# Eleven small loads issued later, and four modulation products put together ahead of a normalisation's turning

## The reference

```
mod = silu(cond) @ w_mod[i] + b_mod[i]          # 1024 -> 6 x 1024, for two conditioning vectors
sh1, sc1, g1, sh2, sc2, g2 = split(mod, 6)
h = modulate(rmsnorm(x, norm1_g[i]), sh1, sc1)
out = hgrn_mixer(h) if i == 0 else fourier_mixer(h)
x = x + g1 * out
h = modulate(rmsnorm(x, norm2_g[i]), sh2, sc2)
x = x + g2 * moe(h)                             # 16 experts, top 2 of one group per token
```

## Time and the profile before

| | us |
|---|---|
| median of 3 runs | 1105.63 |
| lowest and highest | 1104.61, 1108.65 |
| the profiled execution | 1104.64 |
| its span in the trace | 1102.9 |

### The profile page before, as it was taken

The page is one execution under the profiler, slowest core; times in us unless marked ns, Lnnn a source line. Parts: engine busy times, 40 slices in busy tenths (PEclk is TensorE's granted clock), DMA queues, the critical chain, the costliest instruction groups (busy, mean ns, idle before and its releaser), DMA issues.

```text
span 1102.9 us, 17260 instructions
## 1 busy us (share of the span) xinstructions
PE 921.6 (84%) x6701; PEld 510.2 (46%) x6702; DVE 221.1 (20%) x509; ACT 246.4 (22%) x451; POOL 171.1 (16%) x288
## 2 busy tenths in 40 slices
PE   3699999997999965998899997399939999887850
PEld 0345546753446443554455553374425555443420
DVE  1100355201545350000010010601420100000005
ACT  1111123221224131222222221420312222211112
POOL 2001002201001032211121211210211122111112
PEclk9999999999999986999999998699959999999995
DMA  9976464556242975999999983971482999999954
GB/s 380 307 297 230 154 223 163 191 208 248 103 147 94 380 270 199 393 418 418 417 424 421 417 341 142 406 318 62 174 326 87 416 376 420 416 424 422 420 217 170
DMA packets 69227, 320.90 MB, mean 291 GB/s; under 512 B 13252, under 2 KB 15588, under 8 KB 53952
## 3 DMA queue, kind: packets, MB, share of 16 engines
q1 hardware_dynamic: 54592, 290.75, 65.9%
q0 software_dynamic: 9856, 18.51, 4.8%
q10 hardware_dynamic: 4736, 11.01, 2.6%
HBM read 308.70 MB, written 20.53 MB: 299 GB/s over the span
## 4 chain that ended last, share of the span: by engine, by line
PE 36%; DMA 23%; DVE 3%; ACT 3%; issue 2%; SPq 2%; ACTq 0%; POOLq 0%; POOL 0%; DVEq 0%
PE ps L852 13%; PE ps L859 9%; PE ps L749 7%; DMA ring<-in_moe_w_down 7%; DMA deep<-in_moe_w_down 6%; DMA deep<-hrow,gi 3%; DMA ring<-in_moe_w_up 3%; DMA hrow<-deep 2%; SPq L379 2%; DMA yrows<-deep,si 2%; PE ps L828 1%; PE ps L788 1%; PE ps L770 1%; ACT deep L943 1%; DMA deep<-yrows 1%
## 5 line engine op out<-in xcount | busy, mean ns | idle before, releaser
L852 PE MATMUL ps<-ring,deep 128*64 128x256 f32 x1600 | 184.1, 388 | 14.1 <-DMA ring<-in_moe_w_up 10.3
L852 PEld LDWEIGHTS ps<-ring,deep 128*64 128x64 f32 x1600 | 120.1, 140 | 84.7 <-issue 16.7
L571 PE MATMUL ps<-deep,ring 128*128 128x384 f32 x384 | 129.0, 494 | 4.2 <-ACT deep L943 4.2
L1414 DVE TENSOR_TENSOR deep<-deep,ps 128x128 f32<-128x128 f32 x76 | 18.4, 284 | 452.8 <-PE ps L852 452.8
L859 PE MATMUL ps<-ring,deep 128*64 128x512 f32 x400 | 94.7, 617 | 8.3 <-DVE deep L1418 8.3
L571 PEld LDWEIGHTS ps<-deep,ring 128*128 128x128 f32 x384 | 72.6, 192 | 58.9 <-issue 10.5
L852 PE MATMUL ps<-deep 128*64 128x256 f32 x832 | 92.8, 380 | 5.3 <-DMA deep<-in_moe_w_up 4.4
L574 PE MATMUL ps<-ring,deep 128*128 128x512 f32 x192 | 87.9, 610 | 0.0
L749 PE MATMUL ps<-ring,deep 128*128 128x512 f32 x192 | 83.8, 594 | 1.4 <-ACT deep L1023 0.8
L852 PEld LDWEIGHTS ps<-deep 128*64 128x64 f32 x832 | 61.0, 137 | 40.8 <-issue 6.3
L504 PE MATMUL ps<-ring,scond 128*32 128x512 f32 x384 | 52.9, 674 | 21.2 <-DMA ring<-in_w_mod 20.4
(11 more groups left out here) (162 smaller groups left out, 776.9 us busy)
## 6 DMA issues: line engine op xcount, KB each, us to landing
ring<-in_w_mod SPq DMA_DIRECT2D x24, 2048.0 KB, 12.0
ring<-in_moe_w_gate SPq DMA_DIRECT2D x22, 2048.0 KB, 22.9
ring<-in_moe_w_up SPq DMA_DIRECT2D x22, 2048.0 KB, 27.6
ring<-in_moe_w_down SPq DMA_DIRECT2D x22, 2048.0 KB, 32.7
ring<-in_hgrn_w_in SPq DMA_DIRECT2D x10, 2048.0 KB, 8.6
deep<-in_moe_w_gate SPq DMA_DIRECT2D x10, 2048.0 KB, 20.9
deep<-in_moe_w_up SPq DMA_DIRECT2D x10, 2048.0 KB, 25.2
deep<-in_moe_w_down SPq DMA_DIRECT2D x10, 2048.0 KB, 30.8
```

What stands on the lines that cost most here:

```text
L571: last = mm(bank[:, 0:T], W[:, k, b * P:(b + 1) * P], hT[:, k, :], start=(k == 0), stop=(k == KD - 1))
L852: last = mm(ps[g * SLOTS:(g + 1) * SLOTS, GU_BANK[j], 0:2 * P], xt[:, b, h * SLOTS:(h + 1) * SLOTS], slot3(S[j])[:, k, g * F // 2:(g + 1) ...
```

## The change

- `small_loads` is issued behind mod 6 instead of behind hgrn 1.
- mod 20, 21 and 22 go to slots 2, 0 and 1, which hold the weights of experts 1, 4, 7, 10 and 13, and are all issued when fourteen experts are done; mod 23 stays in slot 3 and is issued behind the DFT tables, with no wait of its own.
- The Fourier weights, which take slots 0 and 1, wait for the products of mod 21 and mod 22.
- TensorE runs the four products one after the other ahead of `turn_norm("a1")`, and none inside `fourier`.

```diff
-        for phase, u, s in [("mod", 20, 2), ("mod", 21, 3), ("mod", 22, 2), ("mod", 23, 3), ("four", 0, 0), ("four", 1, 1)]:
+        for phase, u, s in [("mod", 20, 2), ("mod", 21, 0), ("mod", 22, 1), ("mod", 23, 3), ("four", 0, 0), ("four", 1, 1)]:
             place(phase, u, s)
...
                     sp.dma_start(slot3(s), src).then_inc(landed[s], 16)
-                    if u == 1:
-                        small_loads()
                     continue
...
                 mod_load(u)
+                if u == 6:
+                    small_loads()
...
             sp.wait_ge(M[0]["used"], NE - 2)
-            sp.wait_ge(mod_mm, 20)
-            mod_load(20)
-            sp.wait_ge(M[0]["used"], NE)
-            mod_load(21)
+            for u in (20, 21, 22):
+                mod_load(u)
 
             expert_rows(0)
...
-            for U in (22, 23):
-                sp.wait_ge(mod_mm, U - 1)
-                mod_load(U)
+            mod_load(23)
             for u in range(2):
+                sp.wait_ge(mod_mm, 22 + u)
                 s, _ = plan[("four", u)]
                 sp.dma_start(slot3(s), w_o[1][0, :, :, u * C512:(u + 1) * C512]).then_inc(landed[s], 16)
...
                 for t in range(TT):
-                    if t:
-                        mod_gemv(21 + t, 3)
                     for g in range(4):
...
             experts(0)
-            mod_gemv(20, 3)
-            mod_gemv(21, 3)
+            for u in range(20, 24):
+                mod_gemv(u, 3)
             turn_norm("a1", False)
```

## The result

| | before | after |
|---|---|---|
| median, us | 1105.12 (4 runs) | 1094.29 (4 runs) |
| lowest and highest | 1104.11, 1108.65 | 1093.68, 1094.52 |
| the profiled execution | 1104.64 | 1093.68 |
| its span | 1102.9 | 1091.8 |

The ratio is 0.9896, 95% interval 0.9879 to 0.9913: about 11 us faster, where 12.2 were forecast.

A forecast was written before the change was run, and what follows sets the result against it. The chain of waits was taken as the bound, 36% of the span TensorE and 23% transfers. Terms -6.6 + 0.3 - 2.2 - 3.7 = -12.2 us from 1104.64 gave a forecast of 1092.5 us, range 1087 to 1100.

The forecast's parts named there:

- The wait for mod 4: Early projections: mod 4 issued earlier removes TensorE's 5.00 us wait and the slow clock of its product; -6.6 us.
- The small loads elsewhere: SP's queue after mod 6: the eleven small loads cost 4 to 20.3 us there, and nothing on the path.
- Gathers beside mod 21 and 22: Late in the first expert set: gathers beside the earlier loads come slightly late; +0.3 us, bounds 0 and 1.0.
- Scatter and read-back: End of first expert set: with no load issued beside them, last scatter and first read-back finish 4.27 us earlier, bounds 0 and 4.27.
- The estimate of 5.3: Last scatter beside a load, if engines alternate between queues: about twice 2.65 us, making the whole sum 1.2 us smaller.
- The hold: Before the turning: the fourth product waits for mod 23, holding the turning 3.0 us; net -2.2 us at Fourier's start.
- The products out of Fourier: Fourier stage: two products of 1.85 us each leave the chain; -3.7 us, bounds 0 and -3.7.
- rival 3: Turning and after: fourth product brings the clock up (1.7 us), mod 23 lands in time (2.1 more); 1088.7 us, chance 0.08.
- Everything behind moves along: After the early idleness: all that follows moves by its length, stretches bound by expert weights too.

The follow-up runs named there:

- the controls: The changed kernel, unaltered, rerun beside later variants: 1094.29 us (ratio to before 0.9886) and 1093.65 us (0.9898).
- start-only: The kernel before with only the small loads moved behind mod 6: 1099.02 us, ratio 0.9929.
- The two experiments on loads: Kernel before with only the end's loads moved: 1101.25 us; changed kernel with one or two loads again beside the last scatter: 1097.05 and 1099.22 us.
- loads-only: The kernel before with only mod 20 to 23's loads moved, products and small loads where they were: 1101.25 us, ratio 0.9946.

## Why the prediction was right

- **The wait for mod 4 (-6.6).** -6.5 from first to third projection. mod 4 landed 21.2 us after its issue, at 48.3 (47.4 to 48.7 forecast), ahead of 51.99. The third projection came at 53.84, not near 52.4, because the first began 1.3 us late: the third modulation product ran at the low clock (25.77 us, 3.11 for 1.92). This is not the change: three profiles of the changed kernel began their first projection at 38.13, 39.62 and 40.92.
- **The small loads elsewhere (0).** They cost SP 10.3 us, between the bounds of 4 and 20.3, and TensorE waited for neither hgrn 2 nor mod 7.
- **Gathers beside mod 21 and 22 (+0.3).** The first expert set took 249.24 us before and 250.06 after (0.65 of the difference is its first product, 9.54 for 8.89, far ahead of these loads), in the controls 249.38 and 249.76, in the start-only kernel, without these loads, 249.62. No more than a few tenths, and not told from none.
- **Scatter and read-back (-4.27, which the next term contains).** The scatter gave 4.15 (6.50 to 2.35), the read-back's first tile 0.2 (5.1 to 4.9 us to landing). The two experiments on loads show the mechanism from both sides. The Trainium skill ("DMA: Bandwidth & Descriptors", Queues, rings and completion order) has engines taking packets in turn from queues: the scatter with two loads, no longer than with one, agrees. The estimate of 5.3 made from that by equal shares is short of all readings beside one load, 6.50 to 7.29.
- **The hold (-2.2 at Fourier's start).** The fourth product began 18.03 us behind the read-back's issue, 18.2 forecast, and took 3.64 as forecast. The turning began 21.60 behind it for 19.23 before, so it was held 2.4, not 3.0. Fourier began 7.83 us earlier than before by the clock of the trace; less the 5.7 that the last scatter's issue (678.14 to 672.41) was already early, that is 2.1, as against 2.2. Two small errors cancel in this: the read-back was issued 0.3 us earlier than forecast against the end of the expert set (4.15 for 3.85), and Fourier began 0.4 later behind it (27.70 for 27.27), as modulation began 1.21 us behind the turning's start, not 0.75.
- **The products out of Fourier (-3.7).** The term that was mis-sized: Fourier shrank by 5.8. The two products that no longer stand there are 3.7 of it. The rest is the clock: Fourier's first groups ran slow before (5.41 us for the first 16 matmuls) and at the full clock after. I had kept that cost on both sides, and rival 3 had its price (1.7). By the loads-only and start-only kernels the slow clock does not belong to the products' place, so that getting rid of it was luck and is not a gain to count on: in them turning and Fourier together took 22.1 on the mean, so the change is worth 4.8 there and not 6.1. The Trainium skill's rule ("TensorE: Matmul & The Clock Gate", Part 1), by which activity releases a throttled clock, agrees with the turning. Right behind the fourth product the turning took 3.0 to 4.0 us, without it 4.5 to 5.4.
- **Everything behind moves along.** Nearly. The second expert set took 2.2 us longer, of which 1.7 is its last product (5.35 for 3.65), begun after short waits for weights in both kernels. In three profiles of the changed kernel it was 5.35, 5.35 and 3.65, so that this too differs between executions of one kernel. What decides it stays open.

So the mechanism held, for the products' move by the traces alone. The difference between 12.2 and 11.0 lies, in the profiled executions, mostly in the clock at three places: the first projections (+1.3) and the last product (+1.7) against the forecast, Fourier (-1.7 to -2.1) for it.

## What to carry to other kernels

A bulk load issued while a short transfer is on the path can cost that transfer more than its own length again (the scatter took 2.4 to 2.9 us alone, 6.4 to 7.3 beside loads), so what can be loaded earlier into a buffer that has just come free should be. Many small transfers belong behind the next bulk load that something waits for, not ahead of it. Work that must wait for a late load should stand behind the critical step and in the next gap, not ahead of it: here that is worth 1.5 to 1.8 us in the traces, and Fourier ran at the full clock in both kernels that had the product there (10.73 us).

## What the runs showed of the hardware

- The low clock comes and goes at the same place in executions of one kernel: the third modulation product took 1.92, 3.11 and 3.64 us in three profiles of the changed kernel. A few us of difference between two profiled executions can be that alone.
- A gap of 1.91 us ahead of Fourier was followed by a low clock in the kernel before, gaps of 2.14 and 2.38 us in the changed kernel were not. The gap's length alone did not decide it.
- The issue of a load on SP took 19.6 us with five 2 MB loads issued just before it, and 0.37 for the same kind of load later; all that stands behind it on SP waits.
